# First projection pair of each layer from scaled residuals, with mean and deviation put in behind it

## What is computed

```python
for l in range(DEPTH):
    z = x @ w_in                      # split: u_pool, hq, hf, hi, hgate, cq (256), ckv (128), kpe (32), gates
    cq = rms_norm(cq, q_norm)
    ...                               # three mixers, merged to m
    x = layer_norm(DN_ALPHA * x + m @ w_out, ln1_g, ln1_b)
    x = layer_norm(DN_ALPHA * x + conv_ffn(x), ln2_g, ln2_b)
```

## Time and profile before

| | |
|---|---|
| median of 3 runs | 2217.29 us (2217.11 to 2218.4) |
| profiled execution | 2217.46 us, of it the span 2215.7 |
| mean granted TensorE clock | 0.995 |
| HBM | 173.39 MB read, 9.18 MB written, 82 GB/s |

### The profile page before, as it was taken

One profiled execution on the slowest core, in us unless ns is written; L12 is line 12 of the kernel. 1 busy time (PEld: TensorE's weight loads), 2 busy tenths in 40 slices (PEclk: granted clock), 3 DMA queues, 4 the chain that ended last, 5 costly groups with the idle time before them and its releaser, 6 DMA issues.

```text
span 2215.7 us, 37254 instructions
## 1 busy us (share of the span) xinstructions
PE 2177.6 (98%) x11792; PEld 1676.7 (76%) x11792; DVE 1222.6 (55%) x2160; ACT 525.3 (24%) x1116; POOL 1068.3 (48%) x1188
## 2 busy tenths in 40 slices
PE   9999999999999999999899999999999999999996
PEld 6676787777777777777676767777777777777775
DVE  1844675333677666662238447743336776666523
ACT  2453353111141111100125533521111411110002
POOL 4121136576746666624241112456677376665251
PEclk9999999999999999999999999999999999999998
DMA  6222114222132222121132222132221322222211
GB/s 227 95 82 68 43 65 145 77 73 80 58 128 77 76 76 76 70 86 65 39 135 96 72 69 74 65 112 86 86 76 58 110 76 79 84 83 72 79 60 55
DMA packets 53058, 184.60 MB, mean 83 GB/s; under 512 B 7394, under 2 KB 28898, under 8 KB 39330
## 3 DMA queue, kind: packets, MB, share of 16 engines
q1 hardware_dynamic: 52608, 181.31, 23.6%
q10 hardware_dynamic: 290, 1.29, 0.1%
HBM read 173.39 MB, written 9.18 MB: 82 GB/s over the span
## 4 chain that ended last, share of the span: by engine, by line
PE 92%; DVE 4%; issue 3%; ACT 1%; DVEq 0%; DMA 0%; ACTq 0%; SPq 0%
PE ps L1342 26%; PE ps L1224 24%; PE ps L1384 17%; PE ps L942 5%; PE ps L1011 3%; PE ps L974 2%; PE ps L963 2%; PE ps L1550 1%; PE ps L1162 1%; PE ps L1414 1%; PE ps L995 1%; PE ps L1140 1%; PE ps L983 1%; PE ps L1063 1%; PE ps L1026 1%
## 5 line engine op out<-in xcount | busy, mean ns | idle before, releaser
L1342 PE MATMUL ps<-lq,mreg 128*128 128x288 f32 x1008 | 251.3, 406 | 0.0
L1342 PEld LDWEIGHTS ps<-lq,mreg 128*128 128x128 f32 x1008 | 191.5, 190 | 52.9
L1737 ACT ACTIVATE r<-ps 128x288 f32<-128x288 f32 (+7 forms) x264 | 112.8, 431 | 493.6 <-PE ps L1224 256.0
L1342 PE MATMUL ps<-xT,wring 128*128 128x288 f32 x672 | 169.8, 406 | 0.0
L1342 PEld LDWEIGHTS ps<-xT,wring 128*128 128x128 f32 x672 | 127.7, 190 | 35.3
L1224 PE MATMUL ps<-r,kbuf 128*128 128x288 f32 x576 | 143.6, 406 | 0.0
L2946 POOL TENSOR_TENSOR kbuf<-o_mla 128x288 f32<-128x288 f32 x42 | 33.3, 792 | 207.7 <-DVE o_mla L2720 207.7
L1224 PEld LDWEIGHTS ps<-r,kbuf 128*128 128x128 f32 x576 | 109.4, 190 | 30.2
L2073 ACT ACTIVATE r<-r 128x592 f32<-128x592 f32 x44 | 30.7, 697 | 428.2 <-DVE r L2756 428.2
L1224 PE MATMUL ps<-xT,wring 128*128 128x288 f32 x512 | 129.6, 406 | 0.0
L1737 ACT ACTIVATE o_mla<-ps 128x288 f32<-128x288 f32 (+1 forms) x108 | 45.1, 420 | 321.0 <-PE ps L1384 214.5
(11 more groups left out here) (480 smaller groups left out, 4757.4 us busy)
## 6 DMA issues: line engine op xcount, KB each, us to landing
wring<-w_stream SPq DMA_DIRECT2D x98, 1024.0 KB, 4.9
side<-w_stream SPq DMA_DIRECT2D x18, 704.0 KB, 4.5
r<-pages_in SPq DMA_DIRECT2D x80, 128.0 KB, 2.1
vbuf<-w_stream SPq DMA_DIRECT2D x12, 512.0 KB, 3.7
r<-w_stream SPq DMA_DIRECT2D x12, 512.0 KB, 3.6
wring<-w_stream SPq DMA_DIRECT2D x8, 704.0 KB, 4.1
r<-w_stream SPq DMA_DIRECT2D x6, 704.0 KB, 4.1
mreg<-pages_in SPq DMA_DIRECT2D x32, 128.0 KB, 2.0
```

The lines of the kernel that those rows point to most:

```text
L1342: mm = pe.matmul(up_sum[name], ws[:, k * P:(k + 1) * P], xs[:, k, :], start=(k == 0), stop=(k == HK - 1))
L1737: return act.activation(out, in_, func, **more)
```

## The change

Both layers' first pair is computed from y_next, eight buffers with two spare columns each. In layer 1 they hold the raw second residual of layer 0 times the norm's weights g (LN2), and the spare columns hold g and b, so that the product's last two columns are the sums of the weights times g and times b. VectorE then makes (mean * first column - product), multiplies by rstd, and ScalarE adds the second column with the sign turned. In layer 0 the buffers hold x itself, the spare columns are 0, the mean is 0 and rstd 1. Six buffers lie in own_lev, where GpSimd's x sums also go, two in vbuf. x is loaded to the buffers, and VectorE copies it to xT.

```diff
@@ signals and buffers
+FIRST_COUNTS = (32, 32, 32, 64)
+CQ_FIXES = 5
+        y_own = own_lev[:, 0:6 * (T + 2)].rearrange("p (k t) -> p k t", k=6)
+        y_at = 2 * KF * 34
+        y_next = [y_own[:, k, :] for k in range(6)] + [vbuf[:, 0:T + 2], vbuf[:, y_at:y_at + T + 2]]
+        mean_kept, rstd_kept = r1[:, 0:T], r1[:, T:2 * T]
-        y_ready = signal("y_ready", 2 * KD)
+        y_ready = signal("y_ready", 3 * KD + 1)
...
@@ SyncE, start
-                sp.dma_start(xT[:, lo:hi, :], xT_in[:, lo:hi, :]).then_inc(first_ready[i].sem, 16)
+                own = min(hi, 6)
+                sp.dma_start(y_own[:, lo:own, 0:T], xT_in[:, lo:own, :]).then_inc(first_ready[i].sem, 16)
+                for k in range(own, hi):
+                    sp.dma_start(y_next[k][:, 0:T], xT_in[:, k, :]).then_inc(first_ready[i].sem, 16)
@@ SyncE, layer
                 load_after(l, 1, LOAD)
+                load(l, 2)
                 sp.wait_ge(*layer_done.at(l, 5))
...
-                load(l, 2)
                 load_pages(l, 0)
@@ TensorE
-            pe.sem_inc(x_new.sem, KD)
...
-            def x_pair(l, tile, n, first, split=HALF):
+            def y_pair(l, tile, n, split=HALF):
                 for k in range(KD):
                     if k in FIRST_PARTS:
-                        pe.wait_ge(*first_ready[FIRST_PARTS.index(k)].at(l, 32))
-                    pe.wait_ge(*x_new.at(l, first + k + 1))
+                        i = FIRST_PARTS.index(k)
+                        pe.wait_ge(*first_ready[i].at(l, FIRST_COUNTS[i]))
+                    if k in (0, KD - 1):
+                        pe.wait_ge(*y_ready.at(l, KD - 2 + 2 * (k // (KD - 1))))
                     for j in range(2):
                         w = w_slot[n % 2][:, (2 * k + j) * P:(2 * k + j + 1) * P]
-                        for a, (lo, hi) in enumerate(((0, split), (split, T))):
+                        for a, (lo, hi) in enumerate(((0, split), (split, T + 2))):
...
@@ hf_quad, first product of quad 0
-                    pe.wait_ge(*taken_at(l, TILE_CQ + 1))
+                    pe.wait_ge(*ln_centred.at(l, 3))
@@ TensorE, layer
-                x_pair(l, TILE_CQ, 0, 0)
+                y_pair(l, TILE_CQ, 0)
                 pe.wait_ge(*w_ready[1].at(l, 16))
+                pe.wait_ge(*x_new.at(l, KD))
@@ ScalarE
+            def next_residual(l, j):
+                act.wait_ge(*residual_at(l, 1, j))
+                copy(y_next[j][:, 0:T], rT[:, j, :], scale=vec[:, V_LN2G + j:V_LN2G + j + 1]
+                     ).then_inc(y_ready.sem, 1 + (j == KD - 1))
...
+                else:
+                    copy(two(mean_kept), two(ln_slot(0))[:, :, 0:HALF]).then_inc(mean_sq_ready.sem, 1)
                 act.wait_ge(*var_ready.at(l, which + 1))
                 act.activation(rstd, rstd, ACT.Ln).then_inc(logs.sem, 1)
                 act.wait_ge(*logs.at(l, which + 1))
-                act.activation(rstd, rstd, ACT.Exp, scale=-0.5).then_inc(roots.sem, 1)
+                act.activation(two(rstd_kept) if which else rstd, rstd, ACT.Exp, scale=-0.5).then_inc(roots.sem, 1)
...
-                    copy(two(sq_c[j]), halves(TILE_CQ + j), ACT.Square).then_inc(sq_ready.sem, 1)
-                    copy(two(cq[:, j, :]), halves(TILE_CQ + j)).then_inc(tile_act.sem, 1)
+                    copy(first_terms[j], slot(TILE_CQ + j)[:, 512 + HALF:512 + HALF + 2]).then_inc(sq_ready.sem, 1)
+                for j in range(2):
+                    act.wait_ge(*ln_centred.at(l, 4 + 2 * j))
+                    copy(sq_c[j], cq[:, j, :], ACT.Square, bias=first_terms[j][:, 1:2], scale=-1.0).then_inc(sq_ready.sem, 1)
+                    copy(cq[:, j, :], cq[:, j, :], ACT.Identity, bias=first_terms[j][:, 1:2], scale=-1.0
+                         ).then_inc(tile_act.sem, 1)
@@ VectorE, set-up
             dve.wait_ge(lb_ready, 5)
+            for ap in (y_own[:, :, T:T + 2], y_next[6][:, T:T + 2]):
+                dve.memset(ap, 0.0)
+            dve.memset(y_next[7][:, T:T + 2], 0.0).then_inc(y_ready.sem, KD)
+            dve.memset(mean_kept, 0.0)
+            dve.memset(rstd_kept, 1.0).then_inc(ln_centred.sem, 1)
+            for i, count in enumerate(FIRST_COUNTS):
+                dve.wait_ge(*first_ready[i].at(0, count))
+                for k in range(FIRST_PARTS[i], FIRST_PARTS[i + 1]):
+                    dve.tensor_copy(xT[:, k, :], y_next[k][:, 0:T]).then_inc(x_new.sem, 1)
             dve.wait_ge(const_ready, 16)
@@ VectorE, norm: in the second one centre(0) goes behind the variance, and four blocks are centred ahead instead of five
-                for j in range(1, HK + 1):
+                ahead = HK + 1 - which
...
+                for j in range(1 - which, ahead):
@@ VectorE, start of a layer
+                dve.wait_ge(*ln_centred.at(l, 1))
+                for j in range(2):
+                    dve.wait_ge(*sq_ready.at(l, j + 1))
+                    dve.scalar_tensor_tensor(out=two(cq[:, j, :]), in0=two(mean_kept), scalar=first_terms[j][:, 0:1],
+                                             in1=halves(TILE_CQ + j), op0=ALU.mult, op1=ALU.subtract
+                                             ).then_inc(ln_centred.sem, 1)
+                for j in range(2):
+                    dve.wait_ge(*ln_centred.at(l, 2 + j))
+                    dve.tensor_tensor(cq[:, j, :], cq[:, j, :], rstd_kept, ALU.mult).then_inc(ln_centred.sem, 1 + j)
@@ GpSimd, start of a layer
                 pool.wait_ge(*x_new.at(l, KD))
-                for ready in first_ready:
-                    pool.wait_ge(*ready.at(0, 32))
+                pool.wait_ge(*tile_ready.at(l, TILE_CQ + 2))
```

More of the change, by code:

```diff
@@ L925, in _ @@
             sp.wait_ge(y_stored, 16 * (KD // 2))
-            for ready in first_ready:
-                sp.wait_ge(*ready.at(DEPTH, 32))
+            for ready, count in zip(first_ready, FIRST_COUNTS):
+                sp.wait_ge(*ready.at(DEPTH, count))
         @block.tensor
@@ L1777, in scaled_residual, with next_columns @@
                 copy(y_scaled[:, j, 0:T], rT[:, j, :], scale=vec[:, V_LN1G + j:V_LN1G + j + 1]).then_inc(y_ready.sem, 2)
+            def next_residual(l, j):
+                act.wait_ge(*residual_at(l, 1, j))
+                copy(y_next[j][:, 0:T], rT[:, j, :], scale=vec[:, V_LN2G + j:V_LN2G + j + 1]
+                     ).then_inc(y_ready.sem, 1 + (j == KD - 1))
+            def next_columns(l):
+                act.wait_ge(*conv_hist_put.at(l, KF))
+                for to, at in ((T, V_LN2G), (T + 1, V_LN2B)):
+                    copy(y_own[:, :, to], vec[:, at:at + 6])
+                    for k in (6, 7):
+                        copy(y_next[k][:, to:to + 1], vec[:, at + k:at + k + 1])
             def residual_copies(l, which):
@@ L1799, in residual_copies @@
                         scaled_residual(l, 2 * m)
+                    else:
+                        if m == 0:
+                            next_columns(l)
+                        next_residual(l, 2 * m)
                 residual_square(l, which, KD - 1)
+                if which == 1:
+                    next_residual(l, KD - 1)
             def norm_scale(l, which):
@@ L2262, in centre @@
                 def centre(j):
-                    if which == 0:
-                        dve.wait_ge(*y_ready.at(l, 2 * j + 2))
+                    dve.wait_ge(*y_ready.at(l, KD + 2 * j + 2 if which == 0 else 3 * KD + j + 1))
                     return dve.tensor_tensor(two(rT[:, j, :]), two(rT[:, j, :]), mean, ALU.subtract)
@@ L2268, in norm @@
                 dve.wait_ge(*mean_sq_ready.at(l, which + 1))
-                centre(0).then_inc(ln_centred.sem, 1)
+                if which == 0:
+                    centre(0).then_inc(ln_centred.sem, 1)
                 dve.wait_ge(*tile_ready.at(l, tile + 2))
@@ L2278, in norm @@
                 for j in range(KD):
-                    dve.wait_ge(*ln_centred.at(l, which * KD + j + 1))
-                    dve.tensor_tensor(two(rT[:, j, :]), two(rT[:, j, :]), rstd, ALU.mult).then_inc(ln_mul.sem, 1)
-                    if j + HK + 1 < KD:
-                        centre(j + HK + 1).then_inc(ln_centred.sem, 1)
-                        if j + HK + 2 == KD:
+                    dve.wait_ge(*ln_centred.at(l, 1 + CQ_FIXES + which * KD + j + 1))
+                    dve.tensor_tensor(two(rT[:, j, :]), two(rT[:, j, :]), two(rstd_kept) if which else rstd, ALU.mult
+                                      ).then_inc(ln_mul.sem, 1)
+                    if j + ahead < KD:
+                        centre(j + ahead).then_inc(ln_centred.sem, 1)
+                        if j + ahead + 1 == KD:
                             dve.sem_inc(tile_dve.sem, 1)
             with dve.Fori(0, DEPTH) as l:
+                dve.wait_ge(*ln_centred.at(l, 1))
[7 more added lines that the diff above has]
+                    dve.tensor_tensor(cq[:, j, :], cq[:, j, :], rstd_kept, ALU.mult).then_inc(ln_centred.sem, 1 + j)
```

19 lines of the change are left out of this document (11 added, 8 removed).

## The result

| | before | after |
|---|---|---|
| median | 2218.31 us (14 runs) | 2222.61 us (14 runs, 2220.35 to 2224.19) |
| ratio to before | | 1.002, 95% interval 1.0012 to 1.0027 |
| profiled execution | 2217.46 us, span 2215.7 | 2223.59 us, span 2221.8 |

One of the 14 executions of the kernel before took 5158.27 us, the others 2216.61 to 2220.11; without it the median is 2218.26.

A forecast was written before the change was run, and what follows sets the result against it. TensorE, busy 98% of the span, was taken to bound the kernel, leaving only its waits and half-clock time to win. +7.1 (start) -6.1 (border) +0.2 (tail) = +1.2 us on 2217.3 gave 2218.5 us, range 2216.0 to 2221.6.

The forecast's parts named there:

- start: Layer 0's pair: first matmul at 11.75 us instead of 4.23, cold again, pair ending at 30.05 instead of 22.96; +7.1 us.
- border: Between the layers: wait for normalised x goes, 2.4 us gap at full clock, pair ends at 1116.85 instead of 1122.98; -6.1 us.
- behind the pair: Work of VectorE, ScalarE, GpSimd and loads after the first pair: all stays covered by TensorE's products; cost 0.
- tail: Last layer's second norm at the kernel's end: logarithm 0.3 earlier, centrings lose 0.5; +0.2 us (-0.4 to +0.6).
- The hold: Start: layer 0's pair waits for y_ready, raised by VectorE's last memset behind lb_ready; first matmul 7.5 us later.
- the branch: Border: TensorE's branch back, 3.362 us from 1097.5, becomes what is late, so layer 1 is issued only from 1100.9.
- GpSimd's cover: Behind the pair: sums ready 12.1 us after its end, wanted by TensorE's third product at 13.75; margin 1.65 us, cost 0.
- rival 1: Border: the clock falls all the same; price 2.1 us, time 2220.6; chance 0.24.
- Rival 2: Start: not held up, y_ready gets its count with the first data; time 2211.4; chance 0.05.
- Rival 3: Border: the branch costs less in the new order, up to 2.3 us more saved; time 2216.2; chance 0.05.
- Rival 4: Behind the pair: GpSimd's sums stretch beside VectorE's work past the 1.65 us margin; 4.7 in both layers, 2223.2; chance 0.08.

The follow-up runs named there:

- e2: Kernel before, with only the hold: layer 0's pair released by VectorE behind its wait for lb_ready at 5; 2226.75 us, ratio 1.0038.
- e1: Changed kernel with the three spare-column memsets moved ahead of VectorE's wait for lb_ready; 2215.05 us, ratio 0.9985 to the kernel before.
- e12: Same early memsets on the changed kernel as e1, in the last set of runs beside the changed kernel; 2214.19 us, ratio 0.9983 to before.
- The filler: Four unused 512-column products between last sum and branch: on the changed kernel 2220.27 us, ratio 1.001; with early memsets 2212.62 us, ratio 0.9977.
- e4: Early memsets as in e1, and the next layer's pair put at the loop body's end, ahead of TensorE's branch; 2210.26 us, ratio 0.9966.

## Why the prediction was wrong

| term | forecast | measured |
|---|---|---|
| start | +7.1 (6.6 to 7.5) | +7.8 between the profiles; 8.2 alone (e2), 7.6 and 8.4 by its removal |
| border | -6.1 (-4.0 to -8.5) | -3.9 between the profiles; with the tail -3.5 and -4.2 (e1, e12 against before); in the profiles -3.9 to -4.3 with a fall of the clock, -5.8 and -6.0 without |
| behind the pair | 0 | 0, with 1.0 us of margin |
| tail | +0.2 | +0.25 |
| sum | +1.2 | +4.3, +4.2 |

**The waits held, the clock did not, and one size was off.** The hold is where I put it, released by the memset I named; the branch takes the border's wait over; GpSimd's cover holds; the tail is off by 0.05.

**The step that failed: the clock at the border.** "The gap is then 2.4 us, and since the old fall came only 3.7 us in, I take it that the clock stays full." One fall 3.7 us into one gap is no bound for others: in the profiles it came 2.6 to 3.5 us behind the end of the last sum, also where the pair had begun again by then. This was rival 1, with a price of 2.1 us and a chance of 0.24. It came in five of seven profiles, at 1.7 us. Where it came, the border saved 3.9 to 4.3 us; where it did not, 5.8 and 6.0, which is my 6.1. I should have asked for which gaps the rows show a full clock behind them. Rival 1 reads the earlier trace rows wrongly there: the 1.7 us of the third row are the total of four waits, the longest of them 0.6, and no other data wait of TensorE in that profile passes 0.8; so nothing spoke for 2.4. By the mean clock the changed kernel loses some 3.3 us to falls ahead of its last norm, more than the one at the border can cost; the falls within the layers, which the kernel before has too, my sum did not speak of.

The Trainium skill (TensorE: Matmul & The Clock Gate, Why this matters for your kernels) asks for no long idle gaps of TensorE between bursts of matmuls. The filler agrees in kind; but the falls came behind gaps of 2.34 to 2.97 us, shorter than those it warns of.

**The start's size.** I read the arrival of the third part from one execution, 8.85 us, and it was an early one. In the later profiles it landed at 8.9 to 10.3, at 9.2 or later in all but one; in the kernel before at 9.68, and in e2, with no change to the loads, at 9.75. So nothing says that the change delayed it; the row I leaned on did not stand for the run. That is most of the 0.7 to 1.1 us above my 7.1, and puts it above my upper end of 7.5.

**The branch's size** was read from one row as well. It took 3.30 to 3.88 us in the profiles, so -6.1 had 0.5 us of its own uncertainty that I left out. By the Trainium skill's 108 ns (Advanced Engine Details and Errata, Control Flow Timing) the pair would have begun at once; that it takes 3.3 us and more shows in every trace, and only moving work ahead of it (e4) wins the gap.

**The rivals.** Rival 2 (no hold) falls with the first matmul at 12.54 us. Rival 3 (a cheap branch) falls with the rows of every trace. Rival 4 (GpSimd) was right in kind: the sums stretch beside VectorE and use up 0.65 us of the 1.65; what is left still covers them, and they decide only in e4.

**What stays open.** Warming TensorE wins 5.2 to 5.3 us by the medians of both sets of runs. The traces show 1.7 to 2.0 of it, as an earlier end of the first pair; against the changed kernel's three profiles the spans are 1.0 to 5.1 us shorter, part of that by falls within the layers that came in one and not in the other. The mean granted clock, 0.9962 over 11 runs in both sets against 0.9956, makes some 1.4 us of fewer falls probable (an estimate, with the clock known to 0.001); the last 2 us stay unexplained. What makes a gap of 2.4 us, or a wait of 0.8, lose the clock in one execution and not in the next was not found.

## What to carry to other kernels

A new wait needs a giver in the loop's first round: find it, and what stands ahead of it on its engine. Here three memsets of 0.06 us behind an unrelated set-up chain cost 8 us, twice what the whole idea wins, and moving them up makes the change 0.15 to 0.17% faster than before. When a data wait at the end of a loop goes, the branch back is what is left; fill it with the next round's first work. And read arrivals, branches and the clock from several executions before a term with a bound of 0.5 us rests on them.

## What the hardware showed that I had not expected

- VectorE's multiplications with both operands in SBUF took 2.7 us beside GpSimd's sums, 0.75 in the last norm, with no sum beside them; the operations with an operand in PSUM took 0.81 ahead of the sums and 0.82 beside the first. A copy of 128x4 took 2.61. The sums grew from 2.62 to 3.02 and 3.16. The 2.7 is above the 1.82 that I had taken as the worst for work of this size; nothing waited for it. The kernel before had such a row already: a 128x4 TENSOR_SCALAR of VectorE took 2.60 us from 21.42, beside a sum from 21.37. The Trainium skill (GPSIMD Engine Reference, Specifications) says that the two engines contend when VectorE has two SBUF inputs or runs in its two-port mode; the rows of the multiplications agree, and in which mode the 128x4 operations ran no row shows.
- The branch back of this long loop body takes 3.3 to 3.9 us on TensorE; the second branch, which leaves the loop, takes 0.067. On GpSimd the row of the branch itself is short in e4 (0.034 to 0.050 us), and yet its next instruction comes 3.0 us behind it.
- The granted clock falls for 3.4 us within a layer in some executions of most versions, the kernel before included, 1.7 us each time; ten of the eleven such falls came 1.9 to 2.6 us behind the end of one wait of 0.8 us.
